# Input projection of a two-layer encoder: how many units run ahead of the mixers, and how many are woven into them

## The reference, cut to what matters

```
h = rms_norm(x, norm_mix_pre[l])
z = h @ w_in[l]                       # 1024 -> 6144 columns
q_h, f_fw, f_bw, i_h, g_h, q_d, k_d, v_d, gate_a, gate_b = split(z)
a = hgrn2_mixer(q_h, f_fw, f_bw, i_h, g_h, ...)      # 4 heads, gated linear attention, both directions
b = diff_attention(q_d, k_d, v_d, ...)               # 4 heads, softmax attention in 128-query blocks
m = sigmoid(gate_a) * (a @ w_branch_a[l]) + sigmoid(gate_b) * (b @ w_branch_b[l])
x = x + rms_norm(m @ w_out[l], norm_mix_post[l])
```

## Time and profile before

| what | value |
|---|---|
| median of 3 runs | 2528.56 us (2527.02 to 2529.72) |
| span of the profiled execution | 2527.1 us |
| TensorE busy (PE) | 2494.0 us, 99% |
| VectorE (DVE), ScalarE (ACT), GpSimd (POOL) busy | 1698.0, 1196.1, 218.8 us |
| all DMA | 322.00 MB, 127 GB/s on average |

### The profile page before, as it was taken

One profiled execution on the slowest core, in us unless ns is written; L12 is line 12 of the kernel. 1 busy time (PEld: TensorE's weight loads), 2 busy tenths in 40 slices (PEclk: granted clock), 3 DMA queues, 4 the chain that ended last, 5 costly groups with the idle time before them and its releaser, 6 DMA issues.

```text
span 2527.1 us, 40959 instructions
## 1 busy us (share of the span) xinstructions
PE 2494.0 (99%) x16826; PEld 2225.3 (88%) x16826; DVE 1698.0 (67%) x2290; ACT 1196.1 (47%) x1832; POOL 218.8 (9%) x236
## 2 busy tenths in 40 slices
PE   9999999999999999999999999999999999999998
PEld 8888888888899999788888888888888999997886
DVE  4276574344789899878443765743547799998784
ACT  4354453332455655456434544533433555564563
POOL 0011210000200000003110202200002000000031
PEclk9999999999999999999999999999999999999999
DMA  6543433344313233833245434433443233347421
GB/s 205 169 122 126 132 122 108 122 161 167 100 59 97 74 101 114 292 104 130 86 144 161 134 126 122 138 108 125 138 165 100 70 86 90 99 133 267 154 88 59
DMA packets 286809, 322.00 MB, mean 127 GB/s; under 512 B 9760, under 2 KB 217248, under 8 KB 286624
## 3 DMA queue, kind: packets, MB, share of 16 engines
q1 hardware_dynamic: 212192, 162.29, 21.4%
q10 hardware_dynamic: 74432, 157.09, 17.9%
HBM read 254.08 MB, written 65.27 MB: 126 GB/s over the span
## 4 chain that ended last, share of the span: by engine, by line
PE 91%; DVE 4%; ACT 2%; issue 2%; POOL 0%; DMA 0%; SPq 0%; ACTq 0%; POOLq 0%; DVEq 0%
PE ps L989 27%; PE ps L765 21%; PE ps L1161 12%; PE ps L723 5%; PE ps L1267 4%; PE ps L971 4%; PE ps L737 2%; PE ps L1101 2%; PE ps L1127 2%; PE ps L941 2%; PE ps L1247 1%; PE ps L960 1%; PE ps L823 1%; PE ps L883 1%; PE ps L920 1%
## 5 line engine op out<-in xcount | busy, mean ns | idle before, releaser
L989 PE MATMUL ps<-hT_hi,whi 128*128 128x256 f32 (+1 forms) x1280 | 332.6, 342 | 4.9 <-ACT gst L2149 3.5
L1345 DVE TENSOR_TENSOR wlo<-raw,whi 128x2048 fp32r<-128x2048 f32 x77 | 177.7, 2308 | 226.7 <-ACT whi L2042 226.7
L989 PE MATMUL ps<-hT_hi,wlo 128*128 128x256 f32 (+1 forms) x1280 | 327.8, 338 | 0.0
L989 PE MATMUL ps<-hT_lo,whi 128*128 128x256 f32 (+1 forms) x1280 | 327.8, 338 | 0.0
L989 PEld LDWEIGHTS ps<-hT_lo,whi 128*128 128x128 f32 x1280 | 240.8, 188 | 28.8
L989 PEld LDWEIGHTS ps<-hT_hi,whi 128*128 128x128 f32 x1280 | 235.3, 188 | 34.0 <-ACT gst L2149 4.6
L989 PEld LDWEIGHTS ps<-hT_hi,wlo 128*128 128x128 f32 x1280 | 240.6, 188 | 27.3
L765 PE MATMUL ps<-hT_hi,whi 128*128 128x384 f32 x608 | 204.1, 336 | 0.9 <-ACT U L2572 0.6
L765 PE MATMUL ps<-hT_lo,whi 128*128 128x384 f32 x608 | 203.2, 334 | 0.0
L765 PE MATMUL ps<-hT_hi,wlo 128*128 128x384 f32 x608 | 203.1, 334 | 0.0
L1748 DVE TENSOR_TENSOR wlo<-raw,whi 128x1024 fp32r<-128x1024 f32 (+1 forms) x154 | 165.5, 1074 | 42.0 <-ACT whi L2557 42.0
(11 more groups left out here) (289 smaller groups left out, 5843.8 us busy)
## 6 DMA issues: line engine op xcount, KB each, us to landing
raw<-w_up_dram SPq DMA_DIRECT2D x88, 512.0 KB
raw<-w_in_dram SPq DMA_DIRECT2D x64, 512.0 KB
raw<-w_down_dram SPq DMA_DIRECT2D x60, 512.0 KB, 4.4
raw<-w_in_dram SPq DMA_DIRECT2D x16, 1024.0 KB
zT<-hn ACTq DMA_DIRECT2D x40, 384.0 KB, 3.1
zT<-gst ACTq DMA_DIRECT2D x40, 384.0 KB, 2.6
GT<-zT ACTq DMA_DIRECT2D x16, 768.0 KB, 5.5
pD<-CG ACTq DMA_DIRECT2D x26, 384.0 KB, 2.3
```

The costliest lines, as they stand in the source:

```text
L989: ins = mm(ps[:, bank, 0:tn], W[y][:, w[3], w0:w0 + P], hT[x][:, k, t0:t0 + tn], start=(k == 0 and i == 0), stop=(k == KD - 1 and i == 2))
L1345: v.tensor_tensor(wlo[:, g, :], raw[:, s, :], whi[:, g, :].bitcast(F32), ALU.subtract)\
```

## The change

The number of units ahead of the mixers goes from 6 to 12, each head takes three units instead of 4, 4, 4 and 6, and each slot but the first holds exactly one quarter.

```diff
-DENSE = 6
-SIDE = ((6, 10), (10, 14), (14, 18), (18, 24))
+DENSE = 12
+SIDE = ((12, 15), (15, 18), (18, 21), (21, 24))
...
-SLOTS = ((2, 1, 1, 1, 1, 1, 1, 1, 1, 2, 2, 1, 1), (0, 1, 1, 1, 1, 1, 1, 1, 1, 2, 2, 2, 2),
-         (0, 1, 1, 1, 1, 1, 1, 1, 1, 2, 2, 2, 2), (0, 2, 2, 2, 2, 2, 2, 2, 2, 2, 2, 2, 2))
+SLOTS = ((0, 1, 1, 1, 1, 1, 1, 1, 1, 1, 1, 1, 1),) * NH
```

## The result

The changed kernel takes 2536.45 us (median of 5 runs, 2535.6 to 2538.12), the kernel before 2528.56 us (5 runs beside them, 2527.02 to 2529.72). The ratio over all runs is 1.0035, with a 95% interval from 1.0024 to 1.0046: 0.35% slower (the two medians are 0.31% apart). The forecast was 2535.4 us. The profiled run of the changed kernel took 2537.02 us, its span 2535.1. The same file run again beside the later experiments gave 2536.12 us against 2527.22, ratio 1.0035 [1.0023, 1.0048].

What follows compares the result with a forecast made beforehand. TensorE was taken to bound the kernel, busy 2494.0 of 2527.1 us. The terms 7.0 + 2.2 - 1.8 - 0.6 = +6.8 us, added to the 2528.56 us median, gave 2535.4 us, range 2531.5 to 2541.

Steps and rivals of the forecast that it cites:

- Moved work is worth nothing: Quarters cost TensorE the same ahead of the heads (4.245 us) as woven in (4.25 us); only waits can change.
- Part 1, the gap: First head's emptied first slot: TensorE idles 3.5 us per layer before block 1's scores, +7.0 us; bounds 3.2 to 3.9 each.
- The chain of five steps: ScalarE's copy, merged keys, table load and two exponentials in the first head, ending 4.92 us behind the scores' start.
- The rival in which the gap does not open: Block 0's exponentials are done by the diagonal's end, so TensorE does not wait at block 1's scores; 2526.2 us, 4%.
- Part 2, the clock: TensorE falls to half clock behind each layer's new wait at block 1's scores: 1.1 us each, +2.2; bounds 0 and 1.7.
- the forecast's case: Gap of 3.2 to 3.9 us, clock loss of 0.3 to 1.7 us in each layer, 2533 to 2538 us; 57%.
- the rival in which it holds: The gap opens but TensorE stays at 2.4 GHz in both layers: only +4.6 us, 2533.2 us; 20%.
- Part 3, waits that go: TensorE's waits on ScalarE's copies vanish at heads 1 and 2's far blocks (-1.8 us) and head 3's tail (-0.6 us).
- what would show it: Signs at the scores, clock and copies: a 3.2 to 3.9 us wait per layer, PEclk 0.50, three copy waits fewer or shorter.
- Part 4, the thin slots: One-quarter levels and tails cost 0; the second transpose has 1.5 us to spare; bounds 0 to +1.5 us in six tails.
- The rival of the waiting tails: The second transpose waits for VectorE's scaling in each head with a follower: 9 us more, 2544 us, or 2540 at half; 17%.

Runs made afterwards that it cites:

- the last experiment: The changed kernel with head 0's merged keys, block 0 exponentials and diagonal copy put ahead of ScalarE's last copy before the mixers; 2527.12 us against 2526.49, ratio 1.0002.
- The filled gap: The changed kernel with 14 unused identity matmuls between diagonal and block 1 scores in each layer's first head; 2532.00 us against 2526.03 before, ratio 1.0025.
- the one with before's slots: The kernel before with head 0's first slot emptied, its two quarters moved to TAIL + 3 and TAIL + 4; 2539.34 us against 2526.03, ratio 1.0051.
- the experiment: The changed kernel with every head's quarter of TAIL + 3 moved to TAIL + 4; 2566.09 us against 2527.22 for the kernel before, ratio 1.0155.
- two misses: The changed kernel with one quarter in head 0's first slot and none in TAIL + 1 (2532.53 us), or none in level 5 instead (2533.40 us).

## Why the prediction was right, point by point

**Moved work is worth nothing.** Right. TensorE's busy time in the head phases of the last experiment is 497.84 and 608.23 us, that of before 498.00 and 608.48. The same work in other slots takes the same time. With ten or twelve units ahead and the first wait dealt with, the kernel is back at the time of before.

**Part 1, the gap.** Predicted 3.5 us in each layer, +7.0; measured 3.52 and 3.80, 7.3 us. The chain of five steps was the right one, and the shorter copy of the token unit too (0.66 instead of 0.87; the prediction's own proportion gives 0.29 us less, it took 0.2, and 0.21 was measured). The table load lies in the chain without the drain, as the prediction said: the exponential began 0.01 us behind the load's end (226.68 + 1.28 to 227.97). The 0.28 us more in layer 1 lie ahead of the merged keys; what holds ScalarE there the longer was not looked for. The gap was caused by the empty slot and nothing else: before with that slot emptied has the same wait (7.4 us), and the change with the exponentials put first loses it to 3.0. Nothing else was late behind the gap, as said. The rival in which the gap does not open is out with it.

**Part 2, the clock. This is the term that was mis-sized.** Predicted 1.1 us in each layer with a bound of 1.7, +2.2; measured 7.06 - 5.73 = 1.3 us in layer 0 and 8.07 - 5.73 = 2.3 us in layer 1 (the scores at 1486.60, the values at 1494.67), 3.6 together. The busy time of the head phases says the same: 499.21 - 497.84 = 1.4 and 610.53 - 608.23 = 2.3 against the version that keeps the clock. The filled gap gives 3.8 for both. The step that failed is "a whole stretch of that kind loses half of 3.3": the bound came from the one fall in the trace, and I took its length for a fixed one. In layer 1 the half clock lasted some 6.8 us, twice as long, 5.5 of them behind the gap. "Loses half" errs the other way: a stretch at half clock lost less than half of its length, 1.3 of 3.4 us and 2.3 of 5.5. That the clock fell at all, in both layers, was the forecast's case, and the rival in which it holds is out: it did so in both profiles of the change and in the one with before's slots.
The Trainium skill (TensorE: Matmul & The Clock Gate, "Why this matters for your kernels"), which the prediction weighed as speaking against this change, was right in its direction. The gaps that this section warns of are longer than those of 2.11 to 2.70 us behind which the clock fell here, so these runs are stricter than it is. The section gives no price; the runs do, 1.3 to 2.3 us on top of a gap of 3.5 to 3.8 us.

**The clock of before.** Not in the sum at all. The kernel before had a fall of its own in the down product, behind a gap of 2.1 us that the profile calls issue. The profile of the changed kernel has gaps of 1.8 and 1.3 us there and no fall in layer 0, and is 1.8 us shorter in that stage; in layer 1 the stage is 1.7 us longer. The two cancel here by luck. The prediction's sum should have said that about 2 us of either sign come from this stage.

**Part 3, waits that go.** Predicted -1.8 and -0.6. The far blocks (L907, now L906) have no wait left in the list, and the waits on ScalarE's copies went from 1.4 + 3.5 to 4.3 us, -0.6. The two 0.96 us waits and the six of 0.40 us stayed, as said. The idle time of the head phases grew by 2.3 + 2.5 = 4.8 us; 7.3 - 1.9 - 0.6 = 4.8. Under "what would show it" the prediction asked for three waits on the copies fewer or shorter; its own part 3 has two, and two it was.

**Part 4, the thin slots.** Right in what it was for: no wait came in the tail. The slack was sized too small, 1.5 us instead of 2.0, because the prediction let the transpose wait for the last scaling and not for the fourth. With the cover taken away the experiment finds 1.95. The rival of the waiting tails did not occur. In the same breath two misses show that the prediction said too lightly that the tail is the place to check: level 5 and the boundary of halves in the tail also have less cover than a quarter. They held only because the change kept one quarter in each.

**The sum.** Against the profiled span +6.8 was predicted and +8.0 measured. Head phases +8.1: idle +4.8 (predicted 4.6), clock +3.3 to +3.6 (predicted 2.2). The rest of the span has -0.1. By the medians it is +7.9. The interval of the ratio, 0.24% to 0.46%, lies above the 0.2% that the prediction held to be distinguishable.

What stays open: what decides whether the clock falls behind a gap between 2.1 and 3.3 us, and when it sets in. The same code in the same place had a fall of 3.4 us in layer 0 and one of 6.8 in layer 1 in three profiles, and in the run with before's slots 6.8 in both. The length goes with the moment at which the fall sets in (see the last section), but no run was made to set that moment. What makes the issue gaps in the down product was not looked for.

## What to carry to other kernels

Where the bounding engine is busy 98 to 99% of the span, moving its own work about was worth nothing here; what counts is which slot becomes too thin to cover the chain on another engine. List for each slot what ends last there, chain length less cover, and do it again for all slots when an edit shifts which quarter ends a half. By these runs a gap that opens on TensorE is to be charged with its length and, from some 2 us on (2.11 us lost the clock, 1.92 kept it), with a third to two thirds of it again for the clock; and it can be cheaper to change the order on the engine that is waited for than to find useful work for the gap.

## What the runs showed that was not expected

- The granted clock behind every gap of TensorE of 1.4 us or more, in the eleven profiles, in steps of 1 us or finer: behind the 21 gaps of 1.4 to 1.92 us it stayed at 1.00 each time; of the 24 gaps of 2.11 to 3.80 us, 22 had steps at 0.50 behind them. The two that kept it are one of 2.31 us and, in the kernel with the emptied third tail slot, one of 3.24 us ahead of the last tail, though a gap of the same 3.24 us at the same place of layer 0 lost it. So the length of the gap alone does not decide. The half clock lasted some 3.4 us 16 times and some 6.8 us in the other six: five of these are the gap in PRE, one is that of 2.47 us in level 5.
- The long falls are those that set in while TensorE still stood idle. All six began 0.5 to 1.5 us before the gap's end; the 16 short ones began between 0.1 us before it and 1.6 us behind it. In the changed kernel the clock in the gap of layer 0 is still 1.00 at 228.9, that in the gap of layer 1 is 0.50 from 1485.4 on.
- Matmuls that nobody reads kept it: 3.39 us of them, and 1.00 behind.
- A table load did not wait for its instruction's operand. In the last experiment it ran from 221.35 to 222.63, and the exponential that it belongs to began at 225.92. It cost nothing there, since ScalarE would have stood idle; in the changed kernel it is 1.28 of the 4.73 us of the chain.
- Whether a slot needs cover depends on the parity of the quarters ahead of it, since a half is two quarters: with one quarter more in PRE the wait of 3.5 us there was gone, and one of 2.65 us stood in TAIL, eight slots on.
